# Attention scores from rounded and remainder parts of q and k, instead of full-precision products with zero-padded k

## The reference

```python
scores = jnp.einsum('bnqhgd,bnkhd->bnhgqk', qb, kb,
                    preferred_element_type=jnp.float32) * (ATTN_HEAD_DIM ** -0.5)
...
m = jnp.maximum(jnp.max(scores, axis=-1, keepdims=True), sink)
p = jnp.exp(scores - m)
probs = (p / (jnp.sum(p, axis=-1, keepdims=True) + jnp.exp(sink - m))).astype(v.dtype)
```

## Time and profile before

| | before |
|---|---|
| median of 3 executions | 1022.25 us |
| the profiled execution's own time | 1022.76 us |
| its span, first to last instruction | 1020.4 us |
| PE busy | 1009.9 us, 99% |
| DVE busy | 677.4 us, 66% |
| ACT busy | 568.4 us, 56% |
| POOL busy | 67.2 us, 7% |
| granted TensorE clock, mean | 0.998 |

### The profile page before, as it was taken

One profiled execution on the slowest core, in us unless ns is written; L12 is line 12 of the kernel. 1 busy time (PEld: TensorE's weight loads), 2 busy tenths in 40 slices (PEclk: granted clock), 3 DMA queues, 4 the chain that ended last, 5 costly groups with the idle time before them and its releaser, 6 DMA issues.

```text
span 1020.4 us, 15392 instructions
## 1 busy us (share of the span) xinstructions
PE 1009.9 (99%) x5744; PEld 876.5 (86%) x5744; DVE 677.4 (66%) x997; ACT 568.4 (56%) x915; POOL 67.2 (7%) x133
## 2 busy tenths in 40 slices
PE   8999999999999999999999999999999999999997
PEld 7888888887888888888888888998998988888886
DVE  5766765577667766545767764588597666776733
ACT  7645543456565545436555543588668655545542
POOL 0000000111100000000000000404205100000000
PEclk9999999999999999999999999999999999999999
DMA  9666465442546565663665565443242347556521
GB/s 324 216 207 203 165 247 189 147 170 79 162 134 205 167 214 195 213 200 122 192 210 177 181 237 200 130 148 122 84 150 78 125 145 246 166 182 222 211 85 42
DMA packets 124308, 175.81 MB, mean 172 GB/s; under 512 B 7360, under 2 KB 97760, under 8 KB 124256
## 3 DMA queue, kind: packets, MB, share of 16 engines
q1 hardware_dynamic: 121552, 172.77, 50.9%
q10 hardware_dynamic: 2704, 2.33, 0.7%
HBM read 174.02 MB, written 1.06 MB: 172 GB/s over the span
## 4 chain that ended last, share of the span: by engine, by line
PE 92%; ACT 3%; DVE 3%; DMA 1%; issue 0%; SPq 0%; DVEq 0%; ACTq 0%
PE bank L1806 29%; PE bank L1808 14%; PE bank L1732 13%; PE bank L1734 13%; PE bank L1733 13%; PE bank L2134 2%; PE bank L2128 1%; PE bank L1753 1%; PE bank L2032 1%; PE bank L1969 1%; PE bank L1995 1%; ACT w_hi L755 1%; DMA w_raw<-in_ffn_w_gate_up 1%; PE bank L1898 1%; DVE w_lo L1542 0%
## 5 line engine op out<-in xcount | busy, mean ns | idle before, releaser
L1806 PE MATMUL bank<-xT,w_hi 128*128 128x512 f32 x1280 | 444.9, 394 | 0.0
L1187 DVE TENSOR_TENSOR w_lo<-w_raw,w_hi 128x2048 fp32r<-128x2048 f32 x152 | 347.2, 2289 | 107.6 <-ACT w_hi L755 107.0
L755 ACT ACTIVATE w_hi<-w_raw 128x2048 fp32r<-128x2048 f32 x153 | 293.9, 1929 | 118.0 <-PE bank L1734 118.0
L1808 PE MATMUL bank<-xT,w_lo 128*128 128x256 f32 x1280 | 354.8, 277 | 0.0
L1806 PEld LDWEIGHTS bank<-xT,w_hi 128*128 128x128 f32 x1280 | 240.0, 188 | 55.8
L1808 PEld LDWEIGHTS bank<-xT,w_lo 128*128 128x128 f32 x1280 | 240.3, 188 | 0.1
L1732 PE MATMUL bank<-w_hi,hT_hi 128*128 128x512 f32 x352 | 137.5, 391 | 0.0
L1734 PE MATMUL bank<-w_hi,hT_lo 128*128 128x512 f32 x352 | 137.0, 389 | 0.0
L1733 PE MATMUL bank<-w_lo,hT_hi 128*128 128x512 f32 x352 | 137.0, 389 | 0.0
L821 ACT ACTIVATE silu_g<-bank 128x256 f32<-128x256 f32 x80 | 26.3, 382 | 175.3 <-PE bank L1808 175.3
L1277 DVE TENSOR_TENSOR silu_g<-bank,silu_g 128x256 f32<-128x256 f32 x80 | 30.2, 420 | 119.4 <-ACT silu_g L821 119.4
(11 more groups left out here) (316 smaller groups left out, 1215.5 us busy)
## 6 DMA issues: line engine op xcount, KB each, us to landing
w_raw<-in_ffn_w_gate_up SPq DMA_DIRECT2D x170, 512.0 KB, 4.7
w_raw<-in_ffn_w_down SPq DMA_DIRECT2D x88, 512.0 KB, 4.2
w_raw<-in_gdn_w_in SPq DMA_DIRECT2D x32, 512.0 KB, 4.5
w_raw<-in_attn_w_in SPq DMA_DIRECT2D x12, 512.0 KB, 4.3
w_raw<-in_attn_w_out SPq DMA_DIRECT2D x8, 512.0 KB, 4.0
w_raw<-in_gdn_w_out SPq DMA_DIRECT2D x8, 512.0 KB, 4.2
w_raw<-in_ffn_w_gate_up SPq DMA_DIRECT2D x12, 256.0 KB, 5.6
x_sb<-in_x SPq DMA_DIRECT2D x4, 256.0 KB, 5.5
```

What stands on the lines that cost most here:

```text
L755: act.activation(w_hi[u0 % RING][:], w_raw[u0 % RING][:], ACT.Copy).then_inc(hi_ready, 1)
L1187: dve.tensor_tensor(w_lo[u0 % RING][:], w_raw[u0 % RING][:], w_hi[u0 % RING][:].bitcast(F32), ALU.subtract).then_inc(split_ready, 1)
L1806: pe.matmul(banks[m][:], w[0], xT[:, kt, :, :].rearrange("p s n -> p (s n)"), start=(kt == 0), stop=False, skip_group_check=True)
L1808: z = pe.matmul(banks[m][:, 0:SEQ], w[1], xT_hi[:, kt, :], start=False, stop=(kt == KT - 1), skip_group_check=True)
```

## The change

k is written twice side by side into `k_twice` (no zeros), so that its transpose holds the same 64 rows in rows 0 to 63 and 64 to 127. Two k fills are left of four. `kT` keeps a rounded part and a remainder. ScalarE writes the rounded part of one head of q into 64 rows and VectorE the remainder (`q_low`) into the other 64 rows, for each head of the pair, so the sum over 128 rows is (q_hi + q_lo)·k. A score is now four F32R products, two per head: one with k's rounded part (128 keys or 256), one with the remainder. The emptying of a q fill is two instructions on ScalarE and two on VectorE; a fill of that bank and the scores wait for `qk_lo`. VectorE's split of unit `U_ATT` + 5 moves behind the first q tile's bias and rotation and the two `k_low`. The parts of q are ordered anew, and more of them stand ahead of step 0 (9 instead of 6). GpSimd's zeros are gone.

```diff
-Q_BIAS_STEP = [1, 5]
-Q_BEFORE, Q_PARTS = [1, 3, 2], [2, 2, 2, 2, 1, 1]
-FIRST_FILLS = 5
+Q_BIAS_STEP = [2, 5]
+Q_ORDER = [0, 1, 2, 3, 8, 9, 10, 11, 4, 5, 6, 7, 12, 13, 14, 15]
+Q_BEFORE, Q_PARTS = [1, 1, 7], [1, 2, 1, 1, 1, 1]
+FIRST_FILLS = 3
-Q_STEP = {(0, 1): 1, (1, 0): 5, (1, 1): 8}
+Q_STEP = {(0, 1): 1, (1, 0): 4, (1, 1): 8}
+Q_LO_STEP = {(0, 1): 2, (1, 0): 5, (1, 1): 9}
...
-            kzT = sb("kzT", [P, HKV, 2, SEQ], F32, att_mem)
-            qT = sb("qT", [P, PAIRS, SEQ], F32, att_mem)
+            kT = sb("kT", [P, 2, HKV, SEQ], F32R, att_mem)
+            qT = [sb(f"qT{t}", [P, HALF_PAIRS, 2, P], F32R, att_mem) for t in range(TT)]
...
             def q_evac(c, t):
+
                 f = Q_FILL[c, t]
-                att_evac(f, qT[:, 4 * c:4 * c + 4, t * P:(t + 1) * P],
-                         bank[4 + f % 2][:].rearrange("p (k n) -> p k n", k=4))
+                src = bank[4 + f % 2][:].rearrange("p (k n) -> p k n", k=HALF_PAIRS)
+                act.wait_ge(a_fill, f + 1)
+                act.activation(qT[t][0:DH, :, 0, :], src[0:DH], ACT.Copy)
+                act.activation(qT[t][DH:P, :, 1, :], src[DH:P], ACT.Copy).then_inc(a_evac, 1)
...
-            split_lo(U_ATT + 5)
+
+            def k_low(t):
+                dve.wait_ge(a_evac, t + 1)
+                at = slice(t * P, (t + 1) * P)
+                dve.tensor_tensor(kT[:, 1, :, at], bank[4 + t][:].rearrange("p (k n) -> p k n", k=HKV),
+                                  kT[:, 0, :, at].bitcast(F32), ALU.subtract).then_inc(qk_lo, 1)
+
+            def q_low(c, t):
+
+                f = Q_FILL[c, t]
+                src = bank[4 + f % 2][:].rearrange("p (k n) -> p k n", k=HALF_PAIRS)
+                dve.wait_ge(a_evac, f + 1)
+                dve.tensor_tensor(qT[t][DH:P, :, 0, :], src[0:DH], qT[t][0:DH, :, 0, :].bitcast(F32), ALU.subtract)
+                dve.tensor_tensor(qT[t][0:DH, :, 1, :], src[DH:P], qT[t][DH:P, :, 1, :].bitcast(F32),
+                                  ALU.subtract).then_inc(qk_lo, 1)
...
                 dve.wait_ge(q_rot, t + 1)
+                if t == 0:
+                    k_low(0)
+                    k_low(1)
+                    split_lo(U_ATT + 5)
+                    q_low(0, 0)
...
+                for q in Q_LO_STEP:
+                    if s == Q_LO_STEP[q]:
+                        q_low(*q)
                 if s in Q_BIAS_STEP:
...
                 if f >= 2:
                     pe.wait_ge(a_evac, f - 1)
+                for n, q in enumerate(QK_ORDER):
+                    if f - 2 == Q_FILL[q]:
+                        pe.wait_ge(qk_lo, TT + n + 1)
+                if 2 <= f < 2 + TT:
+                    pe.wait_ge(qk_lo, f - 1)
...
-                for half in range(2):
-                    a_fill4(2 * t + half, [k_pad[t][:, 2 * half + m // 2, m % 2, :] for m in range(4)])
+                a_fill4(t, [k_twice[t][:, m].rearrange("p e d -> p (e d)") for m in range(HKV)])
...
-                    pe.matmul(both, qT[:, p, t * P:(t + 1) * P], kzT[:, p // 2, :, 0:keys],
-                              start=(t == 1), stop=True).then_inc(score_done, 1)
+                    for h in range(2):
+                        q = qT[t][:, p % HALF_PAIRS, h, :]
+                        pe.matmul(both[:, h, :], q, kT[:, 0, p // 2, 0:keys], start=(t == 1), stop=False)
+                        z = pe.matmul(both[:, h, :], q, kT[:, 1, p // 2, 0:keys], start=False,
+                                      stop=(t == 1 or h == 1))
+                    z.then_inc(score_done, 1)
```

More of the change, by code:

```diff
@@ L118 @@
 PROBS = 4
-Q_BIAS_STEP = [1, 5]
-Q_BEFORE, Q_PARTS = [1, 3, 2], [2, 2, 2, 2, 1, 1]
-FIRST_FILLS = 5
-Q_STEP = {(0, 1): 1, (1, 0): 5, (1, 1): 8}
+Q_BIAS_STEP = [2, 5]
[4 more added lines that the diff above has]
+Q_LO_STEP = {(0, 1): 2, (1, 0): 5, (1, 1): 9}
+QK_ORDER = [(0, 0), *Q_STEP]
 FILL_ORDER = [f for s in range(STEPS)
@@ L217, in build @@
             b_out = sb("b_out", [P, D], F32, att_mem)
-            k_pad = [sb(f"k_pad{t}", [P, HKV, 2, P], F32, att_mem) for t in range(TT)]
+            k_twice = [sb(f"k_twice{t}", [P, HKV, 2, DH], F32, att_mem) for t in range(TT)]
             v_rows = [sb(f"v_rows{t}", [P, HKV, DH], F32, att_mem) for t in range(TT)]
-            kzT = sb("kzT", [P, HKV, 2, SEQ], F32, att_mem)
-            qT = sb("qT", [P, PAIRS, SEQ], F32, att_mem)
+            kT = sb("kT", [P, 2, HKV, SEQ], F32R, att_mem)
+            qT = [sb(f"qT{t}", [P, HALF_PAIRS, 2, P], F32R, att_mem) for t in range(TT)]
             score_mask = sb("score_mask", [P, P], BF16, att_mem)
@@ L359, in build @@
         a_mask = sem("a_mask")
-        a_zero = sem("a_zero")
+        qk_lo = sem("qk_lo")
         band_split = sem("band_split")
@@ L620, in _ @@
             pool.wait_ge(unit_done, U_ATT)
-            for t in range(TT):
-                z = pool.memset(k_pad[t][:], 0.0)
-            z.then_inc(a_zero, 1)
             pool.tensor_copy(ident_bf[:], ident[:])
@@ L909, in _ @@
                 split_hi(U_ATT + n)
-            for f in range(4):
-                t, half = f // 2, f % 2
-                att_evac(f, kzT[:, 2 * half:2 * half + 2, :, t * P:(t + 1) * P],
-                         bank[4 + f % 2][:].rearrange("p (k e n) -> p k e n", k=2, e=2))
+            for t in range(TT):
+                att_evac(t, kT[:, 0, :, t * P:(t + 1) * P], bank[4 + t][:].rearrange("p (k n) -> p k n", k=HKV))
             def q_evac(c, t):
                 f = Q_FILL[c, t]
-                att_evac(f, qT[:, 4 * c:4 * c + 4, t * P:(t + 1) * P],
-                         bank[4 + f % 2][:].rearrange("p (k n) -> p k n", k=4))
+                src = bank[4 + f % 2][:].rearrange("p (k n) -> p k n", k=HALF_PAIRS)
+                act.wait_ge(a_fill, f + 1)
+                act.activation(qT[t][0:DH, :, 0, :], src[0:DH], ACT.Copy)
+                act.activation(qT[t][DH:P, :, 1, :], src[DH:P], ACT.Copy).then_inc(a_evac, 1)
             def turned(s, ahead):
@@ L1395, in _ @@
             dve.wait_ge(unit_done, U_ATT + 2)
-            dve.wait_ge(a_zero, 1)
             dve.wait_ge(rstd_ready, RSTD_ATT)
@@ L1419, in _ @@
             for t in range(TT):
-                after(row(k_pad[t][:, :, 0, 0:DH], t, 0))
-                after(rotate(k_pad[t][:, :, 0, 0:DH], t, HKV))
-                dve.tensor_copy(k_pad[t][:, :, 1, DH:P], k_pad[t][:, :, 0, 0:DH]).then_inc(k_rot, 1)
+                after(row(k_twice[t][:, :, 0, :], t, 0))
+                after(rotate(k_twice[t][:, :, 0, :], t, HKV))
+                dve.tensor_copy(k_twice[t][:, :, 1, :], k_twice[t][:, :, 0, :]).then_inc(k_rot, 1)
             for t in range(TT):
                 row(v_rows[t][:], t, HKV * DH).then_inc(v_row, 1)
-            split_lo(U_ATT + 5)
+            def k_low(t):
[10 more added lines that the diff above has]
+                                  ALU.subtract).then_inc(qk_lo, 1)
             def q_bias(c, tiles=range(TT)):
@@ L1942, in q_before @@
                 m = sum(Q_BEFORE[:n])
-                q_part(range(m, m + Q_BEFORE[n]))
+                q_part(Q_ORDER[m:m + Q_BEFORE[n]])
             for n in range(2):
@@ L1960, in _ @@
                     t, p = ITEMS[s]
-                    pe.wait_ge(a_evac, Q_FILL[p // HALF_PAIRS, t] + 1)
+                    pe.wait_ge(qk_lo, TT + QK_ORDER.index((p // HALF_PAIRS, t)) + 1)
                     if s >= 2:
@@ L1968, in _ @@
                                   start=True, stop=False)
-                    pe.matmul(both, qT[:, p, t * P:(t + 1) * P], kzT[:, p // 2, :, 0:keys],
-                              start=(t == 1), stop=True).then_inc(score_done, 1)
+                    for h in range(2):
[4 more added lines that the diff above has]
+                    z.then_inc(score_done, 1)
                 if s < len(Q_PARTS):
                     m = sum(Q_BEFORE) + sum(Q_PARTS[:s])
-                    q_part(range(m, m + Q_PARTS[s]))
+                    q_part(Q_ORDER[m:m + Q_PARTS[s]])
                 for n, items in enumerate(FILLS):
```

## The result

| | before | after |
|---|---|---|
| median | 1022.35 us (6 runs, 1021.78 to 1023.25) | 1027.16 us (6 runs, 1025.74 to 1030.75) |
| mean granted clock of these runs | 0.998 (profiled) | 0.993 to 0.999 |
| the profiled execution | 1022.76 us | 1030.75 us, the slowest of the six |

The ratio is 1.0051 (95% interval 1.0041 to 1.0062): slower by 4.8 us, where 2.2 were forecast, and 0.16 us outside the range. The six runs after spread over 5 us: the slowest has the lowest mean clock (0.993), the fastest the highest (0.999), and the four between, 1026.9 to 1027.4 us, have 0.995 to 0.998 in no order. Read the profiled one with that in mind: it is the slowest, some 3.6 us longer than the median.

The account below looks back on a forecast made before the run. TensorE, busy 1009.9 of 1020.4 us, was taken as the bound, with VectorE and ScalarE close behind. Its 4.0 us saving was outweighed by their queues, 2.2 late at step 15: 1022.25 + 2.2 = 1024.5 us, range 1020.0 to 1027.0.

Parts of the forecast that it names:

- TensorE's work: TensorE alone: two k fills less, -0.8 us, and eight tile-1 scores 0.40 cheaper, -3.2; together -4.0.
- the dear product: Rival: F32R product at 128 columns costs 0.22 us, not 0.11; 4.2 to 4.4 late, 1026.5 us; chance 0.20.
- Up to step 0: Before step 0: 0.7 us idle before the first q fill; step 0 starts 0.3 ahead of before, net.
- VectorE's and ScalarE's work: Ten new VectorE subtractions at 0.60 us each, +6.0; ScalarE's copies at 0.49 each, +1.0.
- Steps 0 to 5: Step 4's q fill waits for GpSimd's slow rotation (3.4 us); TensorE idle 2.6, item 5's score 2.5 late.
- Steps 5 to 15: VectorE's and ScalarE's chains make step 11 start 3.0 us late and the turn of step 15 2.2 late.
- Behind it TensorE has no wait to shorten, so this stays to the end: After the turn of step 15: its lateness of 2.2 us stays to the end, giving 1024.5 us.
- VectorE with room to spare: Rival, steps 0 to 9: VectorE's idle time holds the new work, TensorE stays the bound; 1018.9 us; chance 0.15.
- the last steps give back: Rival: VectorE catches up between items 12 and 13, leaving 1.4 us: 1023.7; chance 0.25, shared with too many small waits.

Follow-up runs that it names:

- q's bias early: Changed kernel, output's bias moved from steps 0 to 3 to 11 to 14, q's second-half tile-0 bias from step 2 to 1: 1026.08 us, ratio 1.0035.
- no remainders: Changed kernel without VectorE's remainders of q and k, those halves being zeros: 1022.23 us, ratio 1.0009.
- busy waits: Changed kernel with transposes of the identity into idle banks where TensorE waited in steps 4, 7, 8 and 10: 1025.78 us, ratio 1.0039.
- with the holds taken away: Kernel with q's bias early, its eight q remainders made on all 128 partitions from partition 0: 1025.82 us against 1026.08.
- moved biases and filled waits: Changed kernel with plain tile-0 scores, VectorE's biases in steps 1, 5, 16 to 19, three TensorE pieces moved into waits: 1021.41 us, ratio 0.9989.
- plain scores alone: Changed kernel with plain scores for tile-0 items and no remainders for the two tile-0 q tiles: 1027.20 us, ratio 1.0051.

## Why the prediction was wrong

Two steps failed: a wait was priced at its own length, without the lower clock behind it, and VectorE's and ScalarE's chains were priced too short.

- *TensorE's work*, -4.0: a little too much. Its busy time fell by 2.7 with seven waits in the long stretch (59.45 against 62.14, q's bias early) and by 3.1 with five (59.00, no remainders), so each wait adds about 0.2 of busy time; the product ahead of it counts with its whole duration, 0.39, and not with the 0.23 of a product that another follows. Before has two or three waits there. Less that, the work fell by about 3.6, an estimate. Tile-0 scores were nearly right: 0.60 by the forecast's own way, a step less its parts (223.91 to 225.20, less 0.69), for 0.56, which refutes the dear product. A tile-1 score behind a fill is 0.55 (230.61 to 231.16), not 0.46, and 0.47 elsewhere (260.04 to 260.51); four of the former make the missing 0.4. None of it decides the time, since the other engines' chains end the waits.
- *Up to step 0*: right (0.50 idle for 0.7; item 0 at 8.19 us from the first k fill, forecast 8.06).
- *VectorE's and ScalarE's work*: the term that failed at full clock. "On 64 partitions an instruction is not shorter, its columns are the same" is true, but each of the pair is held until the one before has ended: 1.6 for a pair, not 1.2. ScalarE's copies into the two halves are 0.60 apart, not 0.49. With busy waits (full clock), counted from the first k fill: item 5 at 20.46 (forecast 19.8), turn of step 7 at 26.53 (25.5), item 11 at 32.78 (31.4), turn of step 15 at 44.42 (42.9). The lateness over the forecast grows 0.7, 1.0, 1.4, 1.5, and 1.5 is what this kernel's time shows. Held remainders are only a part of it: with the holds taken away, in the kernel with q's bias early, the turns came 0.7 earlier, through the pairs of steps 2 and 5. ScalarE's two copies in step 8 add 0.2 between the turn of step 7 and item 11 (1.22 for 1.0), an estimate. The other 0.6 lies in small hand-overs of 0.1 to 0.2, for instance between `q_bias` and the rotation; no run takes them apart.
- *Steps 0 to 5*: place, releaser and size of the wait right (2.81 for 2.6); slow rotation right (3.44 for 3.4).
- *Steps 5 to 15*: the waits were where I put them, at the turns and at step 11, behind ScalarE.
- "Behind it TensorE has no wait to shorten, so this stays to the end": the shift stays, 9.3 us at the turn of step 15 and 9.3 at the next stage's first transpose. What the walk left out is the clock. I priced a wait at its own length. In the profiled run TensorE ran at the lower level behind the 2.8 us wait that I had forecast, which made it 0.8 later at the turn of step 7, and again behind the wait of 0.96 at step 11, which made it 4.7 later. In the median it is about 1.1, a difference no larger than the spread of these runs. That a wait takes the clock, and that work in the wait keeps it, is shown clear of the spread in the kernel before (1028.0 against 1025.7), and in the changed kernel by the trace.
- Sum: 2.2 forecast, + 1.5 for the two engines' chains, + 1.1 left for the clock, 4.8 measured.
- The rivals: VectorE with room to spare did not hold, nor did the last steps give back. My slowest case, 1026.5, lay nearest to the measured time, but by luck: its mechanism, the dear product, was wrong.

## What to carry to other kernels

Where one engine is 99% busy, a change that takes work from it and gives it to the next two must be priced by their queues; here 10 VectorE instructions cost 4.9 us and TensorE's saved work was worth nothing until its waits were filled with work that was due anyway. Price a wait of TensorE of 1 us or more at its length and, for some executions, the half clock behind it; in this kernel that was 1.6 to 4.7 us of TensorE's time per phase. Give an engine work only where the form pays: plain scores where 128 columns gain nothing, moved biases and filled waits together turned +4.8 us into -0.8. The plain scores alone gained nothing (1027.20); beside the moved biases and filled waits they were worth 1.5 (1021.41 against 1022.88).
